# Two-layer mixer and expert kernel: the second layer's attention by query tile, with the first tile's output projection and norm inside attention

## What is computed

```python
# modulation: six rows of 1024 per layer and segment, from silu(c) @ w_mod + b_mod
# (shift1, scale1, gate1, shift2, scale2, gate2)
p = softmax(q k^T / 8)                       # two maps per head
a = p[:, 0] - lam * p[:, 1]
o = rms(a @ v) * sub_g * (1 - lam_init)      # rms over 128, per head
x = x + gate1 * (o @ w_o)
h = rms(x) * (1 + scale2) + shift2
q = h @ w_q                                  # 8 expert heads, 2 halves of 128 each
s = q . sub_keys                             # 128 scores per half
# top 16 of each half, top 16 of their 256 sums -> 16 experts per head and token
act = gelu(u_tab[expert] . h); y = sum(softmax(best) * act * v_tab[expert])
x = x + gate2 * y
```

## Time and profile before

| | |
|---|---|
| median of 3 runs | 2826.53 us |
| the profiled execution | 2825.39 us |
| its span | 2823.3 us |
| TensorE busy | 2176.5 us (77%) |
| VectorE busy | 1854.3 us (66%) |
| ScalarE busy | 1162.8 us (41%) |
| GpSimd busy | 1008.8 us (36%) |
| queue of gathers, share of 16 DMA engines | 71.7% |
| longest single item of the chain that ended last | gathers, 15% of the span |

### The profile page before, as it was taken

How to read it: one execution, slowest core, us unless ns; L and a number is a source line. 1 busy time by engine, 2 the same in 40 slices (tenths; PEclk the granted TensorE clock), 3 DMA queues, 4 the chain that set the end, 5 groups by cost and what they waited for, 6 DMA issues and landing times. The chain is left out here.

```text
span 2823.3 us, 39299 instructions
## 1 busy us (share of the span) xinstructions
PE 2176.5 (77%) x13616; PEld 806.7 (29%) x13616; DVE 1854.3 (66%) x4175; ACT 1162.8 (41%) x3330; POOL 1008.8 (36%) x946
## 2 busy tenths in 40 slices
PE   7998999888887776666666678888797777766665
PEld 3334777643222221111111112222253222211111
DVE  3264666647676677767776776875566766766776
ACT  3352333214444443344434465554253344344433
POOL 0011444223444443444343434343103444344442
PEclk9998999999999876667666679999899999876666
DMA  6440000269999999999999999999736999999997
GB/s 263 152 164 30 2 3 2 83 234 375 419 419 419 419 418 420 419 420 419 420 420 420 418 419 419 419 415 401 294 143 266 419 419 419 419 419 420 420 420 329
DMA packets 139463, 933.23 MB, mean 331 GB/s; under 512 B 17676, under 2 KB 18700, under 8 KB 32420
## 3 DMA queue, kind: packets, MB, share of 16 engines
q0 software_dynamic: 115392, 834.78, 71.7%
q1 hardware_dynamic: 23912, 96.26, 8.9%
HBM read 929.88 MB, written 1.10 MB: 330 GB/s over the span
## 5 line engine op out<-in xcount | busy, mean ns | idle before, releaser
L1620 PE MATMUL psum<-ring,diag 64*64 64x512 f32 x6144 | 1079.2, 792 | 520.9 <-ACT diag L1483 520.4
L1440 POOL DMA_INDIRECT ring<-in_uv,experts x768 | 839.6, 1093 | 1289.9 <-PE psum L1620 1092.0
L1835 DVE CUSTOM_DVE_ANT_0 ring<-ring,gate_acc 128x1024 f32<-128x1024 f32 x768 | 941.0, 1226 | 497.4 <-DMA ring<-in_uv,experts 486.8
L1620 PEld LDWEIGHTS psum<-ring,diag 64*64 64x64 f32 x6144 | 201.3, 160 | 1273.6 <-ACT diag L1483 1145.8
L1476 ACT ACTIVATE gel<-dots 128x1 f32<-128x1 f32 x768 | 155.1, 202 | 986.6 <-DVE dots L1835 984.9
L1483 ACT ACTIVATE diag<-eyes,coef 128x64 f32<-128x64 f32 x768 | 267.1, 348 | 71.8 <-ACT coef L1480 0.6
L1480 ACT ACTIVATE coef<-gel,wcur 128x1 f32<-128x1 f32 x768 | 226.1, 294 | 27.8
L446 PE MATMUL psum<-zT,win_ring 128*128 128x512 f32 x368 | 162.9, 599 | 5.2 <-PEq L92 5.2
L2044 PE MATMUL psum<-h_w,yT 128*128 128x512 f32 x256 | 141.2, 647 | 0.0
L1604 PE MATMUL psum<-yT,h_w 128*128 128x512 f32 (+2 forms) x288 | 135.5, 580 | 2.5 <-ACT gate_acc L1519 2.5
L446 PEld LDWEIGHTS psum<-zT,win_ring 128*128 128x128 f32 x368 | 69.5, 192 | 90.6 <-issue 90.6
(11 more groups left out here) (439 smaller groups left out, 2513.4 us busy)
## 6 DMA issues: line engine op xcount, KB each, us to landing
wmod<-in_w_mod SPq DMA_DIRECT2D x16, 1024.0 KB, 10.6
wmod<-in_w_mod POOLq DMA_DIRECT2D x16, 1024.0 KB, 6.5
ring<-in_uv,experts POOLq DMA_INDIRECT x768, 15.5
h_w<-in_w_qkv SPq DMA_DIRECT2D x12, 1024.0 KB, 9.7
win_ring<-in_w_in SPq DMA_DIRECT2D x23, 512.0 KB, 3.5
h_w<-in_w_q SPq DMA_DIRECT2D x20, 512.0 KB, 7.9
scores_qk<-in_w_q SPq DMA_DIRECT2D x18, 512.0 KB
ring<-in_w_mod POOLq DMA_DIRECT2D x8, 1024.0 KB, 9.0
```

The source lines that it names most:

```text
L1440: nc.gpsimd.indirect_dma_start(ring[:, s % RING], None, uv, bass.IndirectOffsetOnAxis(ap=experts[:, n, j:j + 1], axis=0)).then_inc(row_in[ ...
L1620: m = nc.tensor.matmul(ps[(rows, (lower, upper)[r])[c], r], diag[rows, j % DIAGS], ring[rows, j % RING, D + 512 * c:D + 512 * c + 512], st ...
L1835: nc.vector.tensor_tensor_reduce(u, u, hcur[:], 1.0, 0.0, ALU.mult, ALU.add, dots[:, j:j + 1]).then_inc(dot_done, 1)
```

## The change

1. The units of attention go tile by tile (`h, t = u % 8, u // 8`). Scores have two pairs of banks (`DEEP = 2`); banks 4 and 5 (`SPARE`) become free.
2. In units 9 to 15, with the second tile's heads under way, the first tile's o is scaled (unit 9), turned (10), projected (6, 6 and 4 matmuls in 11, 12, 13), gated and added (14), its square is taken and its norm finished (15). After unit 15 `h0` is turned into `oT`. The second tile's o is left unscaled.
3. The chunks 6 and 7 of the modulation leave the tail of attention: `PE_LATE` is now `(0, 1, 6, 7)`, and `LATE_ORDER` has 16 halves, all loaded by GpSimd at the end of layer 0's expert stage. All modulation rows are stored early in attention. SyncE then loads the first two heads' `w_q` (4 x 512 KB) and the gate and norm rows of the first tile, inside attention.
4. The second expert stage begins with the queries. Behind them the second tile's o, scaled at the stage's start, is turned and projected (12 matmuls before row 0, 2 each in rows 1 and 2), gated in row 4, normed in rows 5 and 6 and turned in row 7. The first gathers wait for the ring slots that still hold o (slot 2), h0 (5) and the first `w_q` (6, 7).
5. `ALONE` is 3 for two tiles as well: head 2's query is made for the first tile alone in rows 8 to 12, and again later for the second, so the number of `w_q` halves loaded behind the first six rises from 14 to 16.

The core of the diff:

```diff
-    ALONE = 3 if NT > 2 else AHEAD
+    ALONE, DONE = 3, 1 if ahead else 0
+    if ahead:
+        OUT_AT, MEAN_AT, NORM_AT, TURN_AT, TURNED_AT, PROJECT_AT = {4: 1}, {5: 1}, {6: 1}, {7: 1}, {8: 1}, {1: (1, 6, 7), 2: (1, 7, 8)}
...
+                        if ahead and s == 2:
+                            pool.wait_ge(ot_mm, 1)
+                        if ahead and s == 5:
+                            pool.wait_ge(h_ready, 1)
+                        if ahead and s == RING - 2:
+                            pool.wait_ge(q_mm, 2)
...
-                project(0)
-                project(1, 0, KD // 2)
-                turn(0)
-                pe.wait_ge(ev_done, 2)
-                for head, w in enumerate((w_q, w_f)):
+                if not ahead:
+                    project(0)
+                    project(1, 0, KD // 2)
+                    turn(0)
+                    pe.wait_ge(ev_done, 2)
+                for head, w in enumerate(ahead.w_first if ahead else (w_q, w_f)):
...
+                if ahead:
+                    pe.wait_ge(on_done, 1)
+                    for hd in range(HEADS):
+                        m = nc.tensor.transpose(ps[:, 4 + hd // 4, (hd % 4) * P:(hd % 4) * P + P], ahead.o[:, hd], ident[:])
+                    m.then_inc(ot_mm, 1)
+                    pe.wait_ge(ot_done, 2)
+                    project(1, 0, 6)
...
-    PE_LATE = 2
-    LATE_ORDER = ((2, 0), (2, 1), (0, 0), (3, 0), (3, 1), (0, 1), (4, 0), (4, 1), (1, 0), (5, 0), (5, 1), (1, 1))
+    PE_LATE = (0, 1, 6, 7)
+    LATE_ORDER = ((2, 0), (2, 1), (0, 0), (3, 0), (3, 1), (0, 1), (4, 0), (4, 1), (1, 0), (5, 0), (5, 1), (1, 1), (6, 0), (6, 1), (7, 0), (7, 1))
...
         self.late_groups(pe, 1, 3)
+        self.late_groups(pe, 6, 0)
+        self.late_groups(pe, 7, 1)
...
-    DEEP, TURN, OUT = 3, 6, 7
+    DEEP, SPARE, TURN, OUT = 2, 4, 6, 7
+    SCALE_AT, TURN_O_AT, PROJECT_AT, OUT_AT, MEAN_AT = HEADS + 1, HEADS + 2, {HEADS + 3: (0, 3), HEADS + 4: (3, 6), HEADS + 5: (6, 8)}, HEADS + 6, HEADS + 7
...
-                    h, t = u // 2, u % 2
+                    h, t = u % HEADS, u // HEADS
...
+                    if u == SCALE_AT:
+                        act.wait_ge(var_done, 1)
+                        nc.scalar.activation(ss[:, 0], ss[:, 0], ACT.Sqrt).then_inc(std_done, 1)
...
+                act.wait_ge(mean_done, 1)
+                nc.scalar.activation(ssh[:], ssh[:], ACT.Sqrt).then_inc(root_done, 1)
...
+                    if u == OUT_AT:
+                        dve.wait_ge(gb_in, 48)
+                        dve.wait_ge(proj_mm, 1)
+                        for c in range(2):
+                            cols = slice(512 * c, 512 * c + 512)
+                            tt(h0[:, cols], ps[:, SPARE + c], gate[:, cols], ALU.mult).then_inc(ps_read, 1)
+                        dve.wait_ge(ps_read, 2)
+                        tt(X[:, tile], X[:, tile], h0, ALU.add).then_inc(x_done, 1)
```

More of the change, by code:

```diff
@@ L6 @@
 import math
+from dataclasses import dataclass
 from contextlib import ExitStack
@@ L1356, in out_and_experts @@
         else:
-            w_out = [ahead[0][:, k] for k in range(KD)]
+            w_out = [ahead.w_o[:, k] for k in range(KD)]
         iota = ph.sb("iota", [P, TOPK])
@@ L1547, in _ @@
                 next_h(0)
-                square(1)
-                root(1)
+                if ahead:
+                    act.wait_ge(ot_mm, 1)
+                    for g in range(2):
+                        nc.scalar.activation(yT[:, 4 * g:4 * g + 4, P:2 * P], ps[:, 4 + g].rearrange("p (c t) -> p c t", c=4), ACT.Copy).then_inc(ot_done, 1)
+                else:
+                    square(1)
+                    root(1)
                 act.wait_ge(max_done, 1)
                 nc.scalar.activation(ex[:], best[:], ACT.Exp, bias=nmax[:], accum_out=total[:]).then_inc(exp_done, 1)
-                turned(1)
+                if not ahead:
+                    turned(1)
                 for j in range(TOPK):
-                    if NT > 2 and j in OUT_AT:
+                    if j in OUT_AT:
                         square(OUT_AT[j])
-                    if NT > 2 and j in MEAN_AT:
+                    if j in MEAN_AT:
                         root(MEAN_AT[j])
-                    if NT > 2 and j in TURNED_AT:
+                    if j in TURNED_AT:
                         turned(TURNED_AT[j])
@@ L1587, in _ @@
                 if not after:
-                    with act.Fori((NT - 1) * HEADS, NU) as n:
+                    unit(HEADS, HEADS + AHEAD, 1)
+                    with act.Fori(HEADS + 1, NU) as n:
                         unit(n, None)
@@ new lines, in _ @@
+                    if j in TURN_AT:
+                        if TURN_AT[j] == 3:
+                            pe.wait_ge(q_done, 2 * AHEAD + 2)
+                        turn(TURN_AT[j])
+                    if j in ALONE_QUERY:
+                        pe.wait_ge(ev_done, 2 if ahead else 6)
+                        query(AHEAD, ALONE_QUERY.index(j), 0, 0, KD, 1)
+                    if j in ALONE_SCORE:
+                        if not ahead:
+                            pe.wait_ge(ps_read, 6)
+                        score(AHEAD, ALONE_SCORE.index(j), 0, 1)
@@ L1801, in norm @@
                     tt(h[:, i], h[:, i], bc[:, 0, seg], ALU.add).then_inc(h_done, 1)
-                out(0)
-                mean(0)
-                norm(0)
+                if ahead:
+                    nc.vector.tensor_scalar(ahead.ss, ahead.ss, 1.0 / P, RMS_EPS, ALU.mult, ALU.add).then_inc(var_done, 1)
+                    dve.wait_ge(oroot_done, 1)
+                    ostep(nc.vector.reciprocal(ahead.ss, ahead.ss))
+                    ostep(nc.vector.tensor_scalar(ahead.ss, ahead.ss, 1.0 - LAM_INIT, None, ALU.mult))
+                    tt(ahead.o, ahead.o, ahead.ss.unsqueeze(2).broadcast_to([P, HEADS, P]), ALU.mult).then_inc(on_done, 1)
+                else:
+                    out(0)
+                    mean(0)
+                    norm(0)
                 dve.wait_ge(c_in, 16)
@@ L1811, in _ @@
                     route_part(first, 0, part)
-                out(1)
-                mean(1)
-                norm(1)
+                if not ahead:
+                    out(1)
+                    mean(1)
+                    norm(1)
                 route_part(first, 0, 9)
@@ L2442, in late, with turn_o, project @@
                     m.then_inc(late_mm, 1)
+                def turn_o():
+                    pe.wait_ge(on_done, 1)
+                    for h in range(HEADS):
+                        m = nc.tensor.transpose(ps[:, SPARE + h // 4, (h % 4) * P:(h % 4) * P + P], o[:, 0, h], ident[:])
+                    m.then_inc(ot_mm, 1)
+                def project(k0, k1):
+                    if k0 == 0:
+                        pe.wait_ge(ot_done, 2)
+                    for k in range(k0, k1):
+                        pe.wait_ge(w_o_in[k], 16)
+                        for c in range(2):
+                            m = nc.tensor.matmul(ps[:, SPARE + c], oT[:, k, 0:P], w_o[:, k, 512 * c:512 * c + 512], start=(k == 0), stop=(k == KD - 1))
+                    if k1 == KD:
+                        m.then_inc(proj_mm, 1)
                 scores(0)
@@ L2447, in _ @@
                 late(TURN, range(4))
-                late(OUT, range(4, 6))
+                late(OUT, range(4, 8))
                 for u in range(NU):
```

234 lines of the change are left out of this document (120 added, 114 removed).

## The result

| | before | changed |
|---|---|---|
| median of 7 runs | 2826.44 us | 2837.05 us (2834.37 to 2841.13) |
| span of the profiled execution | 2823.3 us | 2835.2 us |
| ratio to the kernel before | | 1.0038, 95% interval 1.0029 to 1.0047 |

The change costs 10.6 us in the median. The spans of the two profiled executions differ by 11.9 us. 1.3 of those lie ahead of the change: the last transposes of layer 0's heads, which the change does not touch, start at 2032.43 and at 2033.74.

What follows compares the result with a forecast made beforehand. The second expert stage was taken to run at the pace of its DMA gathers, with compute latency deciding before them. -22.7 + 16.2 + 11.1 + 2.5 + 2.0 = +9.1 us gave a median of 2835.6 us, range 2824 to 2842.

Steps and rivals of the forecast that it cites:

- Term 1: Second expert stage's prelude: the first query follows the warming matmuls, 2.25 us after the stage's start instead of 24.94; -22.7 us.
- Term 2: Attention: 13.75 us of projection on a gapless TensorE, units 9 and 10 2.9 us late, tail 0.5 shorter; +16.2 us.
- term 5: TensorE's clock: 3 us lost to slow running before the queries, 1 gained at attention's start; +2.0 us, range -2 to +5.
- that rival: Attention's projection matmuls run at a third of their present time, making attention 9.6 us shorter: 2826.0 us; chance 0.03.
- The drain: ScalarE in attention stands as long again behind each of three table loads (3 x 1.28 us): 2839.4 us; chance 0.03.
- Term 3: End of layer 0's expert stage: four added halves, 1 MB each, delay the last copy to 2046.2 to 2047.2; +11.1 us.
- Term 4: Saturated stretch behind the first gather: two more w_q halves, 1.05 MB at 420 GB/s; +2.5 us.
- the covered projection: Other engines set the pace of attention's units, so TensorE takes in the 13.75 us free: 2821.9 us; chance 0.08.
- the hidden loads: End of layer 0: late loads hide, only TensorE's 4.2 us are added there: 2828.7 us; chance 0.12.
- The slots that would keep the prelude long: First gathers wait for their slots, so the prelude's gain shrinks by up to 5 us: 2840.6 us; chance 0.04.
- the case of both together: TensorE's clock loss at its upper end plus 3 us for gather rows that find no data: 2841.6 us; chance 0.17.

Runs made afterwards that it cites:

- Version 8: Changed kernel with chunks 6 and 7 loaded during attention into dead memory and multiplied in the two waits of its tail; 2821.27 us, ratio 0.9981.
- Version 1: Changed kernel without the four late halves of chunks 6 and 7: not loaded, multiplied or copied; 2825.73 us, ratio 1.0000.
- Version 3: Changed kernel with the output projection inside attention cut from 16 multiplications to 4; 2826.36 us, ratio 1.0001.
- version 2: Kernel before with only chunks 6 and 7 moved from attention to the end of layer 0; 2839.41 us, ratio 1.0048.
- version 4: Changed kernel with the square root of the first tile's head norm in unit 9 replaced by a copy; 2836.09 us, ratio 1.0036.
- version 10: Version 8 without the eight warming multiplications at the start of the second expert stage; 2819.40 us, ratio 0.9979.
- version 12: Changed kernel without the eight warming multiplications at the start of the second expert stage; 2834.61 us, ratio 1.0027.
- version 7: Changed kernel with the four moved halves loaded into ring slots 0 to 3, which are free earlier; 2829.55 us, ratio 1.0015.
- version 11: Version 10 with five idle multiplications of 512 columns in TensorE's first wait in attention; 2821.85 us, ratio 0.9980.
- version 9: Version 7 with the four moved loads issued by SyncE instead of GpSimd; 2836.46 us, ratio 1.0035.
- version 5: Changed kernel with four idle multiplications in each of the two waits of attention's tail; 2836.68 us, ratio 1.0037.
- version 6: Changed kernel without the last two halves of w_q that the second expert stage loads; 2834.82 us, ratio 1.0031.

## Why the prediction was right

It said 2835.6, within 2824 to 2842; it is 2837.05. The main steps came as forecast; one wait was missed, and one small gain came for another reason than the one given. Step by step:

- **Term 1, the prelude (-22.7): right.** Version 8, whose queries run at full clock as those of the kernel before did, has 17.41 us in stretch C against 40.38: -23.0. No gather waited for its slot.
- **Term 2, attention (+16.2): right within 1.1.** Version 1 starts its attention as the kernel before does and takes 81.62 against 65.58: +16.0, of which 0.9 are the turn at half clock and belong to term 5. The transposes of unit 13 come 16.0 us late where 16.7 was forecast, and the tail behind them is as long as before instead of 0.5 shorter, with those 0.9 in it. Version 3 shows the projection on the path. Its 32 records took 5.32 + 5.32 + 3.60 us, that is 0.44 each as in the earlier trace rows. The 131 ns for a sustained matmul of 512 columns that the Trainium skill gives ("TensorE: Matmul & The Clock Gate", "Back-to-back issue gap") are not what these f32 records show, and that rival is out. The drain that the Trainium skill gives behind such a load ("ScalarE: Activation LUTs", "What ACT_TABLE_LOAD costs") is out too: the table load of unit 9 starts at 2088.17 and the root behind it at 2089.47, 1.30 us later.
- **Term 3, the end of layer 0 (+11.1): 2.1 short.** The loads went as forecast: issue at 2035.72, first landing 5.2 us later, each further one 2.5. The last half was multiplied at half clock, so the copy ends at the upper end of the two values given, +11.5. What failed is the silent step behind it, that the barrier stays at 1.4 us. It grew to 3.1, and in all runs with late loads on GpSimd's list the next stage followed the last landing by 5.6 to 5.7 us. The term measures 13.25, alone (version 2) as in the whole.
- **Term 4, bytes (+2.5): right within the spread.** Stretch D averages 683.6 us in those eight executions, and 680.65 in the kernel before and version 2, +2.9 (+3.8 in the changed kernel's own). The late slots that could have added 3 added nothing that shows, though no version tests them alone.
- **Term 5, the clock (+2.0): its size right within 0.6, in part by luck.** The tail's waits do cost: stretch C is 2.3 us longer than in version 8, and the turn 0.9, together 3.2 where 3 was forecast. The gain at attention's start was 1.8 in this execution (79.80 against version 1's 81.62) instead of 1. But the reason given, that the sums of chunks 6 and 7 fill an idle time, is not what brought it: version 1 has the same 16 matmuls there and its first values still take 2.07 us, and in versions 3 and 4, which have them too, the gain is absent. Net +1.4.

-23.0 + 15.1 + 13.25 + 3.8 + 1.4 = +10.55, and 1.3 ahead of the change, is the 11.9 between the spans. This sum closes because the stretches add up; what the versions add is where each part belongs. The barrier in term 3 is the largest miss, and smaller ones of the other sign stood against it; that the total is only 1.5 us off is in part luck. Of the rivals, the covered projection falls with version 3 and the hidden loads with version 1. The slots that would keep the prelude long are out, since the first eight gathers follow one another without a wait for a slot. Half clock was there (3.2 us of it), but stretch D holds no 3 us for late slots, so the case of both together did not come. One reading of mine was wrong and cost nothing: that no compute engine is busy more than three quarters of the time from 2152 us on. In the first window of the earlier trace rows there VectorE is busy 7.62 of 8 us; it holds for the steady rows.

Why a change that halves the prelude loses: it empties attention's tail of work that cost nothing where it stood (stretch B of version 2 is as long without it), and puts it where the next stage waits for it. The prelude's 23 us and the 15 to 16 that attention grows leave some 7 us over, and the bytes and the clock take most of that. Without the moved loads the change breaks even (version 1: 1.0000, with the second gate of layer 1 left incomplete); with that work back in the tail's new waits it wins by 0.19% (version 8).

## What to carry to other kernels

Work that sits in an engine's waits is free only there: before moving it, ask what ends the stage it goes to, and price its loads from the moment their slot comes free, not from their bytes. Moving the first transfer of a saturated stage forward by 20 us is worth about that, but the matmuls that made it late must go somewhere; in a stage where TensorE has no gap they cost their full time again. And waits of 2 us with little between them are worth filling with real work, if it fits: here it took out a stall of 13 us elsewhere, and kept the clock up for the queries, at the price of 1 us in attention's own tail. And a table of stretches misleads where an edit moves the instruction that bounds one: versions 10 and 12 seem to gain 0.5 us more in stretch C than they do.

## What the runs showed of the hardware

- In the eight executions with the moved loads on GpSimd's list, the next phase's first matmul came 5.63 to 5.69 us after the last load had landed, though the last copy had ended 3.0 to 3.3 us before that phase's first instruction on ScalarE, or 3.9 in version 7. Where no load came late (the kernel before, versions 1, 8, 10 and 11), the next phase followed the last copy by 1.4 us. Whether it is GpSimd's queue that is waited for stays open, since version 9 was bound by its copies.
- TensorE's clock at the start of attention differs between executions of the same code there. In the changed kernel and versions 5 and 7 the wait before the first transposes was 2.9 to 3.2 us, and the first values ran in 1.16 us; in versions 3 and 4 the wait was 4.5 us and they ran in 2.08. Versions 6 and 12 lie between (waits of 4.0 and 3.9 us, 1.40 and 1.84 us). In version 3 attention's start, up to the turn of o, was 2.1 us longer than in the changed kernel. In the first group the score matmuls and the sums ahead of the wait had run slower (3.79 and 2.9 to 3.1 us instead of 3.40 and 1.92), which made the wait shorter. A single profile can't price such a place to better than 2 us.
